# A macaron block with split float32 weights: the two parts of each weight side by side instead of in two buffers

## The reference, cut to what matters

```python
x = x + 0.5 * swiglu(rms_norm(x, ffn1_norm), w_gate1, w_up1, w_down1)   # D 1024, D_FF 2816
h = rms_norm(x, mix_norm)
z, xbc, dt_raw, u = split(h @ w_in)                # 1024 -> 1024 + 1536 + 16 + 1024
y_ssd  = ssd_group(z, xbc, dt_raw, ...)            # conv, chunked scan of 16 heads, gate, norm
y_pool = multiscale_pool_group(u, pool_w, pool_scale)
x = x + concat([y_ssd, y_pool]) @ w_out            # 2048 -> 1024
x = x + 0.5 * swiglu(rms_norm(x, ffn2_norm), w_gate2, w_up2, w_down2)
return rms_norm(x, final_norm)
```

## Time and profile before

| | |
|---|---|
| median of 2 timed runs | 1040.05 us (1039.58 to 1040.51) |
| profiled execution, its own time | 1040.21 us |
| its span, first to last instruction | 1038.4 us |
| mean granted TensorE clock | 0.998 |
| TensorE matmuls | 1028.7 us, 4798 recorded |
| TensorE weight loads, beside the matmuls | 847.2 us, 4798 |
| VectorE | 559.5 us, 686 |
| ScalarE | 380.3 us, 489 |
| GpSimd | 178.8 us, 166 |
| HBM read | 96.54 MB |

### The profile page before, as it was taken

One profiled execution on the slowest core, in us unless ns is written; L12 is line 12 of the kernel. 1 busy time (PEld: TensorE's weight loads), 2 busy tenths in 40 slices (PEclk: granted clock), 3 DMA queues, 4 the chain that ended last, 5 costly groups with the idle time before them and its releaser, 6 DMA issues.

```text
span 1038.4 us, 13577 instructions
## 1 busy us (share of the span) xinstructions
PE 1028.7 (99%) x4798; PEld 847.2 (82%) x4798; DVE 559.5 (54%) x686; ACT 380.3 (37%) x489; POOL 178.8 (17%) x166
## 2 busy tenths in 40 slices
PE   9999999999999999999999999999999999999997
PEld 7888888888888878878787888888888888888887
DVE  5544444444344468786799795554444444433442
ACT  6433223323333337652324753432233223333322
POOL 1110111101001132221063452110101101101100
PEclk9999999999999999999999999999999999999999
DMA  6533323322333343222222233333333322233222
GB/s 185 150 113 101 100 86 96 101 83 67 100 99 96 102 128 96 82 81 75 68 81 81 62 102 102 101 102 95 88 100 101 99 87 87 79 110 96 88 65 81
DMA packets 188873, 99.09 MB, mean 95 GB/s; under 512 B 3780, under 2 KB 188200, under 8 KB 188840
## 3 DMA queue, kind: packets, MB, share of 16 engines
q1 hardware_dynamic: 188168, 97.60, 32.4%
q10 hardware_dynamic: 672, 1.05, 0.3%
HBM read 96.54 MB, written 2.10 MB: 95 GB/s over the span
## 4 chain that ended last, share of the span: by engine, by line
PE 95%; DVE 3%; issue 1%; ACT 1%; POOL 0%; ACTq 0%; POOLq 0%
PE bank L1152 29%; PE bank L1154 29%; PE bank L1153 29%; PE bank L1224 1%; PE bank L1218 1%; PE bank L1221 1%; PE bank L1473 1%; PE bank L1475 1%; PE bank L1474 1%; PE bank L1286 0%; PE bank L1308 0%; PE bank L1276 0%; DVE w_lo_part L745 0%; DVE ebuf L905 0%; PE bank L1192 0%
## 5 line engine op out<-in xcount | busy, mean ns | idle before, releaser
L1152 PE MATMUL bank<-xghi,w_hi_part 128*128 128x512 f32 x960 | 377.3, 393 | 0.0
L1154 PE MATMUL bank<-xghi,w_lo_part 128*128 128x512 f32 x960 | 373.7, 389 | 0.0
L1153 PE MATMUL bank<-xglo,w_hi_part 128*128 128x512 f32 x960 | 373.6, 389 | 0.0
L745 DVE TENSOR_TENSOR w_lo_part<-w_raw,w_hi_part 128x1024 fp32r<-128x1024 f32 x194 | 253.9, 1309 | 191.3 <-ACT w_hi_part L500 185.9
L500 ACT ACTIVATE w_hi_part<-w_raw 128x1024 fp32r<-128x1024 f32 x194 | 203.9, 1051 | 194.5 <-PE bank L1154 193.0
L1152 PEld LDWEIGHTS bank<-xghi,w_hi_part 128*128 128x128 f32 x960 | 180.2, 188 | 39.7 <-issue 2.8
L1153 PEld LDWEIGHTS bank<-xglo,w_hi_part 128*128 128x128 f32 x960 | 180.3, 188 | 38.2 <-issue 1.2
L1154 PEld LDWEIGHTS bank<-xghi,w_lo_part 128*128 128x128 f32 x960 | 180.2, 188 | 38.0
L412 POOL TENSOR_TENSOR gate_buf<-gate_buf,rstd 128x512 f32<-128x512 f32 x44 | 56.9, 1294 | 424.4 <-ACT gate_buf L523 424.4
L1152 PE MATMUL bank<-acthi,w_hi_part 128*128 128x512 f32 x330 | 129.0, 391 | 0.0
L1154 PE MATMUL bank<-acthi,w_lo_part 128*128 128x512 f32 x330 | 128.5, 389 | 0.0
(11 more groups left out here) (223 smaller groups left out, 804.2 us busy)
## 6 DMA issues: line engine op xcount, KB each, us to landing
w_raw<-in_ffn_w_gate SPq DMA_DIRECT2D x42, 512.0 KB, 3.8
w_raw<-in_ffn_w_up SPq DMA_DIRECT2D x42, 512.0 KB, 3.8
w_raw<-in_w_in SPq DMA_DIRECT2D x29, 512.0 KB, 3.8
w_raw<-in_ffn_w_down SPq DMA_DIRECT2D x32, 384.0 KB, 3.2
w_raw<-in_ffn_w_down SPq DMA_DIRECT2D x32, 320.0 KB, 3.0
w_raw<-in_w_out SPq DMA_DIRECT2D x16, 512.0 KB, 3.6
out<-xtok SPq DMA_DIRECT2D x4, 512.0 KB, 3.4
xload<-in_x SPq DMA_DIRECT2D x3, 512.0 KB, 7.1
```

Of the source, the lines that this page charges most:

```text
L745: dve.tensor_tensor(wlo[:, slot(m)], raw[:, slot(m)], whi[:, slot(m)].bitcast(F32), ALU.subtract).then_inc(w_lo, 1)
L1152: pe.matmul(bank, w, h, start=first and n == 0, stop=False)
L1153: pe.matmul(bank, w, l, start=False, stop=False)
L1154: mm = pe.matmul(bank, wl, h, start=False, stop=last and n == blocks - 1)
```

## The change

One tile takes the place of two. Its last dimension holds the high and the low part of one weight next to each other; `whi` and `wlo` become views of it with a step of two values (8 bytes). All uses of the two names stay as written. The size is the same: 2 x 16 KB a partition before, 32 KB after.

```diff
@@ -117,8 +117,8 @@
         raw = sb("w_raw", [P, RING, UB, P])
-        whi = sb("w_hi_part", [P, RING, UB, P], F32R)
-        wlo = sb("w_lo_part", [P, RING, UB, P], F32R)
+        woven = sb("w_parts", [P, RING, UB, P, 2], F32R)
+        whi, wlo = woven[:, :, :, :, 0], woven[:, :, :, :, 1]
         xT = sb("xT", [P, DK * S])
```

## The result

The changed kernel takes 1065.74 us (median of two runs, 1065.23 to 1066.24) where the kernel before takes 1040.05: a ratio of 1.0247, with a 95% interval of 1.0203 to 1.0291. It is slower by 25.7 us. The forecast was 1040.5 us, with a range up to 1062.

What follows compares the result with a forecast made beforehand. The prediction took TensorE's nearly gapless matmul stream to bound the kernel; loads, ScalarE and VectorE terms summed 0 + 0 + 0, and with a few tenths for loads it forecast 1040.5 us, range 1037 to 1062 us.

Steps and rivals of the forecast that it cites:

- What bounds the kernel: Whole kernel: a TensorE stream of matmuls with hardly a hole, 4158 steps of 226.7 ns, 943 of 1038.4 us.
- 13.3 ns that stand in each step: Every matmul step: remainder beside 0.417 ns a moving column, from a line through the 512- and 256-wide steps.
- part 2: TensorE's 4290 weight loads, now stepped: taken as 0, bounded by doubled column reading costing 14.1 us in the narrow stream.
- Part 1: Whole kernel: no instructions, waits, DMAs or bytes added or removed, every later tile stays at its place; cost 0.
- rival A: Weight reading doubles and only the last tile's 256-wide matmuls pay: plus 14.1 us, 1054.6 us; chance 0.08.
- The other bound: Weight loads: column reading doubles to 213 ns for 128 columns, free in the wide stream, 14.1 us in the narrow.
- 107 + 13 = 120, just what the narrow stream steps at: Last tile's 256-wide matmuls: reading 128 weight columns, 107 ns, plus 13 ns gives their 120 ns step.
- Parts 3 and 4: 194 ScalarE conversions and 194 VectorE subtractions, stepped: each taken as 0, bounds +0.86 and +1.08 us each.
- D: TensorE's stream disturbed by doubled memory lines touched by loads: 4.3 ns over 4158 steps, 18 us, 1058.5 us; chance 0.06.
- B: Wide stream: load outlasts its covering matmul beyond 213 ns for 128 columns; priced at 295 ns steps, about 1347 us; chance 0.13.

Runs made afterwards that it cites:

- writes-only run: Changed kernel, but TensorE reads each block's 256 values as two packed runs of 128; ScalarE and VectorE still write stepped: 1040.89 us, ratio 1.0004 to before.
- step-4 run: Changed kernel with one buffer written packed, TensorE loading every fourth value of 512 (16 bytes apart): 1090.3 us, ratio 1.0481 to the kernel before.

## Why the prediction was wrong, point by point

**What bounds the kernel** held: the matmul stream is the time, and the step in the loop is the number to watch. The closing sentence named the failure in advance: the step in the loop is no longer that of the moving columns alone.

**"13.3 ns that stand in each step"** is the step that failed, and through it the 0 of part 2. I drew a line through two widths and took the rest for a constant of the matmul. It is not one: over the 213.3 ns of the line's 512 columns it is 2.5 ns (215.8 less 213.3) when the moving side reads one place, 13.3 in the kernel before, 20.0 after the change, and up to 26.7 (240.0) in a constructed case. At 512 columns it depends on how and where the load reads (step, count, place) as long as the moving side goes on through memory, while a packed and a step-2 load take the same 215.8 ns when the moving side stays in place. A shift of the load by 256 bytes brings back what it was at 0. So load and moving columns disturb each other; that they do so by meeting in the same parts of memory is argued, not shown. Both layouts were "213 + something", and the something was assumed not to know of the load.

**Part 1** (no instruction, wait or transfer changes; cost 0) held. It argued that every later tile stays at its place, and looked for a price in size and order alone. That the place of an operand has a price it didn't see.

**Part 2** gave the load 0, on the ground that half its cover was unused. The cover was real: the load's own pace fell only from 111.8 to 118.6 ns, the narrow tile stayed at 120 ns and rival A's 14.1 us didn't come. But cover was the wrong question: the load cost time under matmuls that covered it. The measured term is 6.67 ns x 4158 = 27.7 us. The other bound was wrong too: a load at half pace, counted as free in the wide stream, took 235 ns there at step 4. And "107 + 13 = 120, just what the narrow stream steps at" was a coincidence: the load alone paces at 111.8 ns, and the 120 are those of 256 moving columns. The rule that this part takes from the Trainium skill stands on its page, SBUF — State Buffer, in "Specifications (TRN2)" and not in the section named. By it the load keeps its pace, which nearly held (118.6 ns against 111.8); the loss came from elsewhere.

**Parts 3 and 4.** VectorE 0 as taken. ScalarE +80 ns a conversion, a tenth of the bound, and hidden, as the writes-only run shows.

**The rivals.** D came nearest and had 0.06: TensorE's stream is disturbed, as loads and moving reads come from one memory. Its reason, a doubled number of lines touched, did not hold: a load of one single value gave 231.7 ns, and a packed load 64 bytes later, which touches as many lines as before, 233.2. Its term was mis-sized: 4.3 ns a step from the earlier trace rows, 18 us, where 6.7 ns and 26 us came. That row already showed that the same load under the same columns can take 231 ns, so that 226.7 is not fixed; it should have been read as the width of an unknown and not as a mild disturbance. With D at 240 ns as its upper end the range would have reached 1040 + 55. B's point, a doubled load, was met in the step-4 run: 235 ns and 50 us, near its threshold and far from the 295 ns of its price.

**The span.** 27.7 us were to come and 26.0 came. The two traces, matched matmul by matmul (both have the same 4798), show where the rest went. From one start to the next the 4158 wide ones grew by 26.1 us in all: by 6.7 ns each in the first feed-forward, 6.4 in the second, 5.8 in the first units and only 5.5 in the mixer, where the step before was already 230 to 234 ns in the scan and where one gap before the scan's L1308 shrank from 0.80 to 0.32 us.

What stays open is the mechanism below the addresses. The runs show that a shift of 256 bytes changes nothing and that the difference between the loads vanishes when the moving side stays in place. They don't show whether the distance of the two operands or the place of each counts, which part of the memory the two readers meet in, what the moving side would take with no load beside it (every matmul here has one), nor why the stream settles at 226.7 or 233.3 ns at some places and at other values up to 240 at others.

## What to carry to other kernels

Where matmuls follow each other without a gap, the place of the stationary and the moving operand (here modulo 256 bytes) is a tuning parameter worth 2 to 3% in this kernel, and any change of layout moves it: compare layouts only after trying a few offsets of each. Here a step of 8 bytes between float32 weights slowed the load's own pace by 6% (111.8 to 118.6 ns), and a step of 16 bytes halved it (233 ns). A remainder left over by a fit through two widths is not a constant until something other than the width has been varied.

## What the runs showed of the hardware that I had not expected

- With 512 moving columns that aren't stepped, the distance between matmuls ranged from 215.8 ns (one column, or four neighbouring ones, repeated) through 226.7 (packed, as in the kernel before) to 240.0 (step-2 load, 32 columns repeated), with the clock granted in full.
- A smaller load is not a cheaper one: 128, 96, 64 and 32 packed weight columns gave 226.7, 229.8, 230.3 and 231.5 ns, and one weight value read 128 times gave 231.7.
- Moving columns with a step of 8 bytes take twice as long, 453 ns for 512, while a load with the same step nearly keeps its pace (118.6 ns against 111.8).
- ScalarE's copy of 1024 values into places 8 bytes apart takes 1127 ns against 1047 packed; VectorE's subtraction, which reads one operand and writes with that step, takes 1226 either way.
